# Attention decays of a decoder step, split into a high and a low part for the sums of later keys

## The chip, the cores and the metric

One core of one Trainium2 chip runs the whole step as one program. The metric is the device time of an execution in microseconds, as a median over runs; lower is better. The core has five engines with a queue each, worked off in order: TensorE (PE: matrix products, with its weight loads as PEld), VectorE (DVE), ScalarE (ACT), GpSimd (POOL) and SyncE (SP, which here only issues transfers). They meet only at semaphores: an instruction that waits holds up all that stand behind it in its queue. Transfers of all issuers run on the same 16 DMA engines.

## The reference, cut to what matters

The step has two layers with three sub-layers each. The change lies in the attention of the first layer's middle sub-layer: stick-breaking attention of 8 heads over 512 prompt tokens, computed in causal blocks of 128, and of 8 sample tokens over 512 cached keys.

```python
z = einsum('bqhd,bkhd->bhqk', qb, kb) * scale + bias
log_1m = where(mask, log_sigmoid(-z), 0.0)          # the decay of a key is -log_1m = softplus(z)
log_w = log_sigmoid(z) + cumsum(log_1m, axis=3, reverse=True) - log_1m
w = where(mask, exp(log_w), 0.0)
outs.append(einsum('bhqk,bkhd->bqhd', w, vb))
```

So a key's log weight is z less the sum of the decays of this key and all later ones that the query sees.

## The kernel before

A head's scores lie with the keys on the partitions and the queries along the free axis. Of the 4x4 blocks of 128 keys by 128 queries, 10 are causal, so a head is a tile of 128 x 1280 in four pieces: 512, 384, 256 and 128 columns for key block 0, 1, 2 and 3. Four such tiles hold scores (`ZS`: ZA to ZD) and four hold decays and later weights (`SP`: SA to SD); head h uses tile h % 4. The work goes in pairs of heads, t = 0 to 3.

What is done with a head, engine by engine:

- PE, `scores(t, j)`: products of keys and queries into PSUM bank 0, one piece j after the other.
- DVE, `scored` and `biased` (L1056): scale and bias into the tile in `ZS`. POOL, `masked` (L1223): the diagonal block's mask. DVE, `sized` (L1096): -|z| of the whole tile, from pair 1 on.
- ACT, `decay_of_pair` (L898): exp; after a change of function table, `log` (L902): ln(1 + x); after another change, `weights` of the pair before (L906).
- DVE, `softplus` (L1062): max(z, 0) plus that logarithm. The tile in `SP` now holds the head's decays, and semaphore `sp_done` says so.
- PE, `sums(h, i)` (L791, L794): for piece i, the product of the decays with the triangle `TRI` (keys of this block that are not before the key) and with `ONES` for each later block, summed in one of two halves of PSUM bank 1. Both operands are fp32. A half is taken again once DVE has read it (`lw_done`).
- DVE, `log_weights(h, i)` (L1069): z less the sum, in place. ACT, `weights(h)` (L906): exp into `SP`. PE, `values(t)` (L809): product with V for a pair. ACT, `outputs` (L952) and DVE, `low` (L1100): that product as a high part and a rest, since all large products of the program use operands of the kind float32r, split in two (weights: ACT L2142 makes the high part, DVE L2316 the rest; product L2030).

The loops at the end of `even_pe`, `even_act` and `even_dve` fix by hand in what order each engine does this. For each pair t the queue of ACT reads: outputs of pair t-1, the exps of pair t+1, table, the logarithms of pair t+1, table, the weights of heads 2t and 2t+1. Softplus(2t+2) and softplus(2t+3) stand on DVE among the log weights of head 2t+1. Heads 0 and 1 are started ahead of the loop.

Between these lie, on PE, the attention over cached values (`values_past`, L660, pages fetched by POOL, L1231), and 16 blocks of the adaLN product (L1964), two after each head of most, each of which needs a 512 KB tile AW that SP fetches when the block two before it is done (L633). SP also writes the new keys and the pooling rows out (`even_sp`, L625: 1 MB of keys, then 512 and 4096 pieces of 15 numbers), after it has asked for the first three units of the next stage ("evout").

## Time and profile before

| what | value |
|---|---|
| median of 3 runs | 2434.2 us (2428.53 to 2434.48) |
| span of the profiled execution | 2428.7 us |
| PE busy | 2382.6 us, 98% of the span |
| ACT busy, DVE busy | 995.2 us (41%), 1241.6 us (51%) |
| granted TensorE clock, mean | 0.996 of full |
| the stretch with the changed work | about 565 us to 656 us of the span |

The profiled execution stands at the lower end of the three runs, 5.5 us below their median. The page's view in 40 slices has PE at 9 tenths or more in all but the first and the last slice. Inside the attention stretch the shares differ: in the ten slices of 10 us from 560 to 660 PE is busy for 8.5 to 10.0 of 10 us, DVE for 3.0 to 7.6 and ACT for 2.5 to 8.2.

### The profile page before, as it was taken

What the parts mean: (1) busy time and instruction counts of PE and PEld (TensorE: products, weight loads), DVE (VectorE), ACT (ScalarE), POOL (GpSimd) and SP (SyncE); (2) the same over time, 40 slices, a digit from 0 to 9 for tenths busy, and PEclk for the clock granted to TensorE, in tenths of its full rate; (3) what the DMA queues carried; (4) which work ended last, traced back from release to release, by engine and by line L of the source; (5) the groups of instructions that cost most, each with busy time, mean ns of one, the idle gap of its engine ahead of it and who ended that gap; (6) DMA issues with size and microseconds to landing.
All of it is one profiled execution on the core that took longest, in us unless ns stands there. A gap on an engine that the chain in (4) does not pass through costs nothing.

```text
span 2428.7 us, 43792 instructions
## 1 busy us (share of the span) xinstructions
PE 2382.6 (98%) x18794; PEld 2185.1 (90%) x18794; DVE 1241.6 (51%) x1725; ACT 995.2 (41%) x1399; POOL 115.2 (5%) x232
## 2 busy tenths in 40 slices
PE   6999999999999999999999999999999999999998
PEld 5999999965599999999999999887777999999998
DVE  5533346755576333367533347755554758633245
ACT  4522234625466222346522235533223546522243
POOL 0000000122100000000000000012222100000000
PEclk9999999999999999999999999999999999999999
DMA  8555345774536653565754255544555455632254
GB/s 306 175 184 189 114 158 179 254 216 126 189 118 226 217 165 99 185 208 174 264 181 164 83 167 183 190 157 162 172 165 165 133 177 181 206 129 88 87 179 155
DMA packets 122658, 417.09 MB, mean 172 GB/s; under 512 B 23386, under 2 KB 27610, under 8 KB 122210
## 3 DMA queue, kind: packets, MB, share of 16 engines
q1 hardware_dynamic: 89538, 302.08, 38.8%
q10 hardware_dynamic: 17568, 61.87, 7.2%
q0 software_dynamic: 15360, 50.34, 6.3%
q8 instruction: 149, 2.44, 0.4%
q14 instruction: 43, 0.35, 0.0%
HBM read 390.84 MB, written 23.41 MB: 171 GB/s over the span
## 4 chain that ended last, share of the span: by engine, by line
PE 87%; DVE 5%; DMA 3%; ACT 3%; issue 2%; SPq 1%; POOLq 0%; POOL 0%; ACTq 0%; DVEq 0%
PE PS L2030 71%; PE PS L1425 3%; PE PS L1964 2%; PE PS L1994 2%; DVE WL L2316 2%; PE PS L1355 1%; DMA RAW<-in_w_in 1%; ACT WH L2142 1%; PE PS L1309 1%; PE PS L1340 1%; PE PS L1350 1%; PE PS L1321 1%; PE PS L791 1%; PE PS L1404 1%; PE PS L794 1%
## 5 line engine op out<-in xcount | busy, mean ns | idle before, releaser
L2316 DVE TENSOR_TENSOR WL<-RAW,WH 128x1024 fp32r<-128x1024 f32 (+1 forms) x478 | 633.1, 1325 | 648.7 <-ACT WH L2142 648.0
L2030 PE MATMUL PS<-HH,WH 128*128 128x260 f32 x3432 | 796.5, 285 | 2.4 <-ACT SG L2262 0.7
L2030 PE MATMUL PS<-HH,WL 128*128 128x260 f32 x3432 | 786.5, 283 | 0.0
L2030 PE MATMUL PS<-HL,WH 128*128 128x260 f32 x3368 | 769.6, 283 | 0.0
L2142 ACT ACTIVATE WH<-RAW 128x1024 fp32r<-128x1024 f32 (+1 forms) x478 | 542.0, 1135 | 424.7 <-PE PS L2030 264.9
L2030 PEld LDWEIGHTS PS<-HH,WH 128*128 128x128 f32 x3432 | 569.9, 188 | 24.7 <-issue 16.8
L2030 PEld LDWEIGHTS PS<-HH,WL 128*128 128x128 f32 x3432 | 569.4, 188 | 0.0
L2030 PEld LDWEIGHTS PS<-HL,WH 128*128 128x128 f32 x3368 | 557.0, 188 | 0.6 <-issue 0.2
L2030 PE MATMUL PS<-GH,WH 128*128 128x260 f32 x1408 | 386.1, 284 | 0.2
L2030 PE MATMUL PS<-GL,WH 128*128 128x260 f32 x1408 | 384.2, 283 | 0.0
L2030 PE MATMUL PS<-GH,WL 128*128 128x260 f32 x1408 | 383.5, 283 | 0.0
L2030 PEld LDWEIGHTS PS<-GH,WH 128*128 128x128 f32 x1408 | 259.0, 188 | 2.8 <-issue 2.6
L2030 PEld LDWEIGHTS PS<-GH,WL 128*128 128x128 f32 x1408 | 259.1, 188 | 0.0
L2030 PEld LDWEIGHTS PS<-GL,WH 128*128 128x128 f32 x1408 | 258.9, 188 | 0.2
L2265 ACT ACTIVATE GH<-SQ 128x260 fp32r<-128x260 f32 (+1 forms) x118 | 62.3, 528 | 374.1 <-DVE SQ L2486 374.1
L2486 DVE TENSOR_TENSOR SQ<-SG,PS 128x260 f32<-128x260 f32 (+1 forms) x118 | 65.6, 556 | 164.3 <-PE PS L2030 163.4
L2262 ACT ACTIVATE SG<-PS 128x260 f32<-128x260 f32 (+1 forms) x118 | 57.9, 491 | 219.2 <-PE PS L2030 215.9
L2475 DVE TENSOR_TENSOR GL<-SQ,GH 128x260 fp32r<-128x260 f32 (+1 forms) x118 | 66.3, 562 | 57.6 <-ACT GH L2265 56.9
L2030 PE MATMUL PS<-OGL,WH 128*128 128x260 f32 x256 | 69.6, 282 | 0.0
L1964 PE MATMUL PS<-AW,CSP 128*32 128x256 f32 x1024 | 66.9, 383 | 0.7 <-DMA AW<-in_w_ada 0.7
L1879 POOL DMA_DIRECT2D SR<-in_ret_past x32 | 18.3, 571 | 952.7 <-DVE WL L2316 929.3
L1964 PEld LDWEIGHTS PS<-AW,CSP 128*32 128x32 f32 x1024 | 30.4, 109 | 23.7 <-issue 2.3
(338 smaller groups left out, 2320.0 us busy)
## 6 DMA issues: line engine op xcount, KB each, us to landing
RAW<-in_w_in SPq DMA_DIRECT2D x236, 512.0 KB, 3.6
RAW<-in_w_out SPq DMA_DIRECT2D x120, 704.0 KB, 4.0
AW<-in_w_ada ACTq DMA_DIRECT2D x114, 512.0 KB, 5.6
RAW<-in_w_odd SPq DMA_DIRECT2D x60, 512.0 KB, 3.7
RAW<-in_w_odout SPq DMA_DIRECT2D x30, 512.0 KB, 3.8
RAW<-in_w_even SPq DMA_DIRECT2D x28, 512.0 KB, 4.3
KV<-in_v_pages POOLq DMA_DIRECT2D x32, 256.0 KB, 5.0
SR<-in_ret_past POOLq DMA_DIRECT2D x32, 256.0 KB, 3.9
```

What stands on the lines that cost most here:

```text
L791: last = nc.tensor.matmul(PS[1][:, i % 2, 0:LEN[i]], TRI[:], SP[h % 4][:, OFF[i]:OFF[i] + LEN[i]], start=True, stop=(i == 3))
L794: last = nc.tensor.matmul(PS[1][:, i % 2, (j - i) * P:LEN[i]], ONES[:], SP[h % 4][:, OFF[j]:OFF[j] + LEN[j]], start=False, stop=(j == 3))
L1425: last = nc.tensor.matmul(PS[tt // 2 if full else 0][:, tt % 2, :], src[k][:, tt // 2, (tt % 2) * P:(tt % 2 + 1) * P], w[:, w0:w0 + RV], s ...
L1964: last = nc.tensor.matmul(ADAP[CG * j:CG * j + CG, int(g == 1), 0:2 * P], CSP[:, k, :], w[:, 2 * P * j:2 * P * j + 2 * P], start=(k == 0), ...
L1994: last = nc.tensor.matmul(ps[:, x, 0:HT], w[:, k * P:(k + 1) * P], src[k][:, x, :], start=(start and k == 0), stop=(stop and k == KC - 1))
L2030: last = nc.tensor.matmul(ps[:, x, 0:HT], w[:, k * P:(k + 1) * P], src[k0 + k][:, x, :], start=(begin and t == 0), stop=(end and t == 2))
L2142: nc.scalar.activation(parts(p)[0], RAW[:, from_:from_ + w], ACT.Copy).then_inc(hi_done, 1)
L2262: nc.scalar.activation(SG[:, s, hs], PS[0][:, hs, 0:HT], ACT.Silu).then_inc(gate_evac, 1)
L2265: nc.scalar.activation(GH[:, r // 2, hs], G32[:, s, hs], ACT.Copy).then_inc(gh_done, 1)
L2316: nc.vector.tensor_tensor(low_, RAW[:, from_:from_ + w], high_.bitcast(F32), ALU.subtract).then_inc(lo_done, 1)
L2475: nc.vector.tensor_tensor(GL[:, r // 2, hs], G32[:, r // 2 % 2, hs], GH[:, r // 2, hs].bitcast(F32), ALU.subtract).then_inc(gl_done, 1)
L2486: nc.vector.tensor_tensor(G32[:, s, hs], SG[:, s, hs], PS[1][:, hs, 0:HT], ALU.mult).then_inc(up_evac, 1)
```

## The change

Each head's decays are written a second and a third time: ACT copies them to a tile of kind float32r (`high_part`, tiles SHA and SHB in turn), and DVE writes decays less high part, over the decays themselves and also as float32r (`low_part`). `sums` then makes each product twice, with the high and with the low part, both operands float32r: `TRIR` and `ONESR` are copies of the triangle and the ones, made once by ACT. The sums wait for `spl_done` (low part) where they waited for `sp_done` (softplus).

The tiles SHA and SHB take the place of the pooling inputs, so ACT's first high part waits until these are written out (`pool_out`), and SP writes them out before it asks for the first "evout" unit, not after the third. The four transfers have a semaphore of their own, so DVE no longer waits for the write of V before it fills ZC. OS, PSC and PT move to other addresses.

```diff
@@ even_sp
             for i in range(len(STEPS["evout"])):
-                if i == 3:
+                if i == 0:
                     sp.wait_ge(ev_act, EV_FULL)
                     sp.wait_ge(ev_dve, EV_FULL)
...
-                        sp.dma_start(dst, src).then_inc(out_done, 16)
+                        sp.dma_start(dst, src).then_inc(pool_out, 16)
+                if i == 3:
@@ even_pe, sums
                 if i == 0:
-                    pe.wait_ge(sp_done, h + 1)
+                    pe.wait_ge(spl_done, h + 1)
+                if h + i == 0:
+                    pe.wait_ge(const_ok, 3)
...
-                last = nc.tensor.matmul(PS[1][:, i % 2, 0:LEN[i]], TRI[:], SP[h % 4][:, OFF[i]:OFF[i] + LEN[i]],
-                                        start=True, stop=(i == 3))
-                for j in range(i + 1, 4):
-                    last = nc.tensor.matmul(PS[1][:, i % 2, (j - i) * P:LEN[i]], ONES[:],
-                                            SP[h % 4][:, OFF[j]:OFF[j] + LEN[j]], start=False, stop=(j == 3))
+                for j in range(i, 4):
+                    w = TRIR if j == i else ONESR
+                    for x, part in enumerate((SPH[h % 2], SPL[h % 4])):
+                        last = nc.tensor.matmul(PS[1][:, i % 2, (j - i) * P:LEN[i]], w[:],
+                                                part[:, OFF[j]:OFF[j] + LEN[j]], start=(j == i and x == 0),
+                                                stop=(j == 3 and x == 1))
@@ even_act
+            def high_part(h):
+                act.wait_ge(sp_done, h + 1)
+                if h == 0:
+                    act.wait_ge(pool_out, 64)
+                after(act, s_done, 4 * (h - 2) + 4)
+                nc.scalar.activation(SPH[h % 2], SP[h % 4], ACT.Copy).then_inc(sph_done, 1)
...
             table(EXP_SET)
+            act.wait_ge(kv_used, 4)
+            act.wait_ge(ident_ok, 4)
+            for dst, src in ((TRIR, TRI), (ONESR, ONES)):
+                nc.scalar.activation(dst[:], src[:], ACT.Copy).then_inc(const_ok, 1)
...
+            high_part(0)
             table(EXP_SET)
             decay(1)
...
-                for h in (2 * t, 2 * t + 1):
-                    weights(h)
+                if t == 0:
+                    high_part(1)
+                weights(2 * t)
+                if t < 3:
+                    high_part(2 * t + 2)
+                weights(2 * t + 1)
+                if t < 3:
+                    high_part(2 * t + 3)
@@ even_dve
+            def low_part(h):
+                dve.wait_ge(sph_done, h + 1)
+                nc.vector.tensor_tensor(SPL[h % 4], SP[h % 4], SPH[h % 2].bitcast(F32),
+                                        ALU.subtract).then_inc(spl_done, 1)
...
                     if t == 1:
-                        dve.wait_ge(out_done, 96)
+                        dve.wait_ge(pool_out, 64)
...
             nc.vector.tensor_tensor(ZN[:, 0, :], ZN[:, 0, :], PS[2][:, 0, :], ALU.subtract).then_inc(zn_dve, 1)
+            low_part(0)
             scored_one()
...
                 log_weights(2 * t, 1)
+                if t:
+                    low_part(2 * t + 1)
                 scored(t + 1, 2)
...
                 if t == 0:
                     softplus(1)
+                    low_part(1)
...
                 if t < 3:
                     softplus(2 * t + 3)
+                    low_part(2 * t + 2)
```

The queue of ACT around pair 0, before (SC_119 is the tile SC; L898 is an exp, L902 a logarithm, L906 a head's weights):

```order
L898 ACTIVATE SC_119<-SC_119 128x1280 [waits z_dve]
L898 ACTIVATE SD<-SD 128x1280 [waits z_dve]
L2166 ACT_TABLE_LOAD
L902 ACTIVATE SC_119<-SC_119,ONES 128x1280 [waits e_done]
L902 ACTIVATE SD<-SD,ONES 128x1280 [waits e_done]
L2166 ACT_TABLE_LOAD
L906 ACTIVATE SA<-ZA 128x1280 [waits lw_done]
L906 ACTIVATE SB<-ZB 128x1280 [waits lw_done]
```

And now (L909 is the exp, L913 the logarithm, L921 a high part, L925 the weights):

```order
L909 ACTIVATE SC_119<-SC_119 128x1280 [waits z_dve]
L909 ACTIVATE SD<-SD 128x1280 [waits z_dve]
L2208 ACT_TABLE_LOAD
L913 ACTIVATE SC_119<-SC_119,ONES 128x1280 [waits e_done]
L913 ACTIVATE SD<-SD,ONES 128x1280 [waits e_done]
L2208 ACT_TABLE_LOAD
L921 ACTIVATE SHB<-SB 128x1280 [waits sp_done]
L925 ACTIVATE SA<-ZA 128x1280 [waits lw_done]
L921 ACTIVATE SHA<-SC_119 128x1280 [waits s_done,sp_done]
L925 ACTIVATE SB<-ZB 128x1280 [waits lw_done]
L921 ACTIVATE SHB<-SD 128x1280 [waits s_done,sp_done]
```

The high part of head 1 (SHB<-SB) stands behind both exps, both logarithms and both table loads of pair 1, and those of heads 2 and 3 stand before and behind the weights of head 1.

The queue of DVE at the end of pair 0, before (L1062 is softplus, L1069 the log weights of a piece):

```order
L1062 SCALAR_TENSOR_TENSOR SB<-ZB,SB 128x1280 [waits z_dve,l_done]
L1069 TENSOR_TENSOR ZB<-ZB,PS 128x512 [waits s_done]
L1069 TENSOR_TENSOR ZB<-ZB,PS 128x384 [waits s_done]
L1062 SCALAR_TENSOR_TENSOR SC_119<-ZC,SC_119 128x1280 [waits z_dve,l_done]
L1069 TENSOR_TENSOR ZB<-ZB,PS 128x256 [waits s_done]
L1069 TENSOR_TENSOR ZB<-ZB,PS 128x128 [waits s_done]
L1062 SCALAR_TENSOR_TENSOR SD<-ZD,SD 128x1280 [waits z_dve,l_done]
```

And now (L1093 softplus, L1098 the low part, L1105 the log weights):

```order
L1093 SCALAR_TENSOR_TENSOR SB<-ZB,SB 128x1280 [waits z_dve,l_done]
L1098 TENSOR_TENSOR SBL<-SB,SHB 128x1280 [waits sph_done]
L1105 TENSOR_TENSOR ZB<-ZB,PS 128x512 [waits s_done]
L1105 TENSOR_TENSOR ZB<-ZB,PS 128x384 [waits s_done]
L1093 SCALAR_TENSOR_TENSOR SC_119<-ZC,SC_119 128x1280 [waits z_dve,l_done]
L1105 TENSOR_TENSOR ZB<-ZB,PS 128x256 [waits s_done]
L1105 TENSOR_TENSOR ZB<-ZB,PS 128x128 [waits s_done]
L1093 SCALAR_TENSOR_TENSOR SD<-ZD,SD 128x1280 [waits z_dve,l_done]
L1098 TENSOR_TENSOR SCL<-SC_119,SHA 128x1280 [waits sph_done]
```

A low part stands directly behind the softplus of head 1 and waits there for ACT; that of head 2 stands behind the softplus of head 3.

SP's queue, before and now in one piece:

```order
-L1916 DMA RAW<-in_w_evout 128x1024 [waits lo_done] x3
-L625 DMA out_k_t<-KP 128x2048 [waits ev_dve,ev_act]
-L625 DMA out_k_t<-QKVS 128x32
-L625 DMA out_pool_p<-UP 512x1x15
-L625 DMA out_pool_n<-US 4096x1x15
+L632 DMA out_k_t<-KP 128x2048 [waits ev_dve,ev_act]
+L632 DMA out_k_t<-QKVS 128x32
+L632 DMA out_pool_p<-UP 512x1x15
+L632 DMA out_pool_n<-US 4096x1x15
+L1957 DMA RAW<-in_w_evout 128x1024 [waits lo_done] x3
```

The four transfers now stand ahead of the three units of "evout".

## Rows read from the trace of the kernel before

**Rows 1.** The page: busy time, share and instructions; then shares of the chain that ended last.

```profile
PE 2382.6 (98%) x18794; PEld 2185.1 (90%) x18794; DVE 1241.6 (51%) x1725; ACT 995.2 (41%) x1399; POOL 115.2 (5%) x232
...
PE 87%; DVE 5%; DMA 3%; ACT 3%; issue 2%; SPq 1%; POOLq 0%; POOL 0%; ACTq 0%; DVEq 0%
```

**Rows 2.** Timeline of PE, sums of head 3: start us, us, engine, line, operation, form, count.

```profile
605.18 1.12 PE L791 MATMUL PS<-SD,TRI 128*128 128x512 f32 x2
...
609.87 0.38 PE L1976 MATMUL PS<-IDENT,ADS 128*128 128x128 f32 x2
```

**Rows 3.** Timeline of PE: neighbouring float32r products of 512 and of 260 columns.

```profile
538.14 0.39 PE L753 MATMUL PS<-WH,HH 128*128 128x512 f32 x1
538.37 0.39 PE L753 MATMUL PS<-WH,HL 128*128 128x512 f32 x1
...
657.39 0.28 PE L2030 MATMUL PS<-OHB,WH 128*128 128x260 f32 x1
657.51 0.28 PE L2030 MATMUL PS<-OLB,WH 128*128 128x260 f32 x1
```

**Rows 4.** The page: splitting a weight tile of 1024 columns (busy, mean ns of one).

```profile
L2316 DVE TENSOR_TENSOR WL<-RAW,WH 128x1024 fp32r<-128x1024 f32 (+1 forms) x478 | 633.1, 1325 | 648.7 <-ACT WH L2142 648.0
...
L2142 ACT ACTIVATE WH<-RAW 128x1024 fp32r<-128x1024 f32 (+1 forms) x478 | 542.0, 1135 | 424.7 <-PE PS L2030 264.9
```

**Rows 5.** Timeline of ACT: the weights of head 0, and the last table loads of pairs 1 and 2.

```profile
589.51 1.27 ACT L906 ACTIVATE SA<-ZA 128x1280 f32<-128x1280 f32 x1
...
610.03 1.28 ACT L2166 ACT_TABLE_LOAD   x1
...
632.04 1.28 ACT L2166 ACT_TABLE_LOAD   x1
```

**Rows 6.** Timeline of DVE: a softplus and the first steps of a later pair.

```profile
588.66 1.48 DVE L1062 SCALAR_TENSOR_TENSOR SC<-ZC,SC 128x1280 f32<-128x1280 f32 x1
...
601.34 1.51 DVE L1096 SCALAR_TENSOR_TENSOR SA<-ZA 128x1280 f32<-128x1280 f32 x1 [0.27 <-DVE ZB L1056]
...
623.35 1.51 DVE L1096 SCALAR_TENSOR_TENSOR SC<-ZC 128x1280 f32<-128x1280 f32 x1 [0.19 <-issue]
```

**Rows 7.** Timeline of PE: where heads 1, 2, 4 and 6 start their sums.

```profile
584.43 1.13 PE L791 MATMUL PS<-SB,TRI 128*128 128x512 f32 x2 [0.99 <-DVE SB L1062]
...
591.28 1.12 PE L791 MATMUL PS<-SC,TRI 128*128 128x512 f32 x2
...
611.37 1.10 PE L791 MATMUL PS<-SA,TRI 128*128 128x512 f32 x2
...
633.86 1.10 PE L791 MATMUL PS<-SC,TRI 128*128 128x512 f32 x2 [0.34 <-DVE ZB L1069]
```

**Rows 8.** Timelines of PE and SP, and a window with DMA share and GB/s last.

```profile
541.50 3.61 PE L646 MATMUL PS<-PAGE,QBM 128*16 128x512 f32 x16 [1.11 <-DMA PAGE<-in_k_pages]
...
532.87 1.11 SPq L625 DMA_DIRECT2D out_pool_n<-US  x1
...
542.00:544.00 2.00, 2.00 (x12) 0.51 (x10) 0.74 (x1) 0.00 (x0) 0.36 (x1) 1.00 1.69 102
```

**Rows 9.** Timeline of PE, and windows with the granted clock third from the end.

```profile
24.18 4.38 PE L1964 MATMUL PS<-AFIRST,CSP 128*32 128x256 f32 x48 [2.88 <-DMA AFIRST<-in_w_ada]
...
35.01 1.21 PE L1994 MATMUL PS<-HH,WH 128*128 128x260 f32 x4 [3.22 <-ACT HH L2201]
...
24.50:25.00 0.50, 0.50 (x8) 0.20 (x4) 0.00 (x0) 0.00 (x0) 0.00 (x0) 0.50 1.03 410
...
27.50:28.00 0.50, 0.50 (x16) 0.29 (x12) 0.00 (x0) 0.00 (x0) 0.00 (x0) 1.00 0.98 393
...
40.50:41.00 0.50, 0.50 (x4) 0.50 (x4) 0.06 (x1) 0.07 (x1) 0.00 (x0) 0.50 0.92 270
```

**Rows 10.** Timeline of PE: the adaLN block after head 6, and the next stage's first product.

```profile
642.49 0.64 PE L1964 MATMUL PS<-AW,CSP 128*32 128x256 f32 x8 [0.73 <-DMA AW<-in_w_ada]
...
656.21 0.39 PE L2030 MATMUL PS<-OHB,WH 128*128 128x260 f32 x1
```

More of the change, by code:

```diff
@@ L476, in decoder_step @@
         TRI = at("TRI", [P], g); g += size([P])
+        OS = at("OS", [4, NS], g); g += size([4, NS])
+        PSC = at("PSC", [4], g); g += 64
+        PT = at("PT", [NS * PAGES], g, I32); g += size([32])
         up_at = g
@@ L970, in even_act @@
             table(ROOT_SET)
-            act.wait_ge(out_done, 96)
+            act.wait_ge(pool_out, 64)
+            act.wait_ge(out_done, 32)
             for q, (n, hs) in enumerate(STEPS["evout"]):
@@ L1947, in _ @@
                 sp.dma_start(y_t[:, g:g + n, HT * x:HT * x + HT], X[:, g:g + n, x, :]).then_inc(y_out, 16)
-            sp.wait_ge(out_done, 96)
+            sp.wait_ge(pool_out, 64)
+            sp.wait_ge(out_done, 32)
             sp.wait_ge(rp_out, 32 * RH)
```

28 lines of the change are left out of this document (16 added, 12 removed).

## The prediction, made before the changed kernel ran

> **What bounds the kernel now.** I read the page first. PE is busy 98% of the span and makes 87% of the chain that ended last, with 5% on DVE and 3% on ACT [rows 1]. So over the whole program a shorter product is worth its time. Then I took the attention stretch apart with the timelines of PE, DVE and ACT side by side, since there a head passes through all three before PE can take its sums. What the reader should see there is how narrow PE's lead is: head 1's sums start after 0.99 us idle for a softplus, head 6's after 0.34 us idle for DVE [rows 7]. Each head's sums begin almost as soon as its decays are there. Whatever is put between softplus and sums lies on the path at once.
>
> **What is taken from PE.** The sums of head 3 run without a wait from 605.18 to 609.87, 4.69 us for 2560 columns [rows 2]; fp32 products show as two instructions each (x2). A float32r product of 512 columns takes 538.37 - 538.14 = 0.23 us, one of 260 columns 0.12 us [rows 3], so 0.45 ns per column. High and low part make 5120 columns: 2.3 us. A head gains 4.69 - 2.3 = 2.4 us of PE, eight heads 19 us. No row has a float32r product under 260 columns, and the sums have 8 of 128 columns per head. Bounds: 0.06 us (in proportion to columns) up to 0.12 us, what 260 columns take; times 64 such products that is 0 to 3.8 us over all heads, and also a price beyond that can't be excluded. I take 0.1 us each, most of which falls into time in which PE waits anyway: 0.5 us on the path.
>
> **What is put on ACT and DVE.** High part: ACT reads and writes 1280 elements per partition; the weights of a head, of that size, take 1.27 us [rows 5]. Low part: a DVE operation of two inputs with 1280 elements takes 1.48 us [rows 6]; splitting a weight tile of 1024 costs 1.14 us on ACT and 1.33 us on DVE in the page's mixed means [rows 4], so both are near 1.3 and 1.5 us. Eight of each are 10 us of ACT and 12 us of DVE. Between them lie only semaphores, some 0.05 us each. If everything stood free, a head's sums would start 1.3 + 1.5 = 2.8 us later. But the queues decide. I walked them pair by pair, with rows' durations and the new order.
>
> Head 0. The copies of V end at 566.9, the high part ends near 568.2 and the low part near 569.7. It stands ahead of the four scalings of head 1, which go back by 1.6 us. The wait for the write of V that DVE no longer has gives back 0.8 us, and PE's shorter sums absorb the rest: softplus(1) ends where it did, near 584.3. The 2.4 us of head 0 are gone. The copies of triangle and ones (two of 128 columns, under 0.3 us each) fall into 0.6 us in which ACT waits for DVE; without that cover they would cost 0.5 us.
>
> Head 1. Its decays are ready at 584.4 [rows 7]. But its high part stands behind the exps, table, logarithms and table of pair 1, and ACT is free at 589.5 [rows 5]. High part until 590.8, low part until 592.3: the sums start at 592.3 and not 584.4, **7.9 us late**. Behind DVE's wait stand the log weights of head 1 and the softplus of heads 2 and 3, so these can't run ahead either.
>
> Pair 1. softplus(2) started at 588.66 [rows 6], 4.2 us after head 1's sums; with shorter sums this becomes 2.7 us, so 595.0. softplus(3) follows 2 us later and ends near 598.4, then DVE makes low(2) until 599.9, and head 2's sums start at 599.9 instead of 591.28 [rows 7]: 8.7 us late.
>
> Pair 2. The first -|z| of head 4 was at 601.34 [rows 6], 10.1 us after head 2's sums. The gain of PE there is eaten by low(3), 1.4 us ahead of two scalings: 609.8, 8.5 us late. ACT follows this through exps, table, logarithms and table, which ended at 610.03 + 1.28 = 611.3 [rows 5], now 619.8. Before the high part of head 4 come the weights of head 2: 1.2, then 1.3 and 1.5 us for high and low part. Head 4's sums start near 623.8 instead of 611.37 [rows 7]: **12.4 us late**.
>
> Pair 3. The same: the -|z| of head 6 (623.35 [rows 6], 12.0 us after head 4's sums) comes 11 us after them, since copies that held it up now fall into PE's wait: 11.5 us late. The table load that ended at 632.04 + 1.28 = 633.3 [rows 5] ends at 644.8, plus 1.2 + 1.3 + 1.5 gives 648.8 for head 6's sums instead of 633.86 [rows 7]: **15 us late**.
>
> The end. From there PE needed 22.4 us to the next stage at 656.21 [rows 10]. Two heads save 4.8 us, less 1.4 us for low(7), and PE waits for the adaLN tile, 0.73 us now [rows 10], some more then, since the tile's transfer doesn't get shorter. Net 2.8 us back: **+12.2 us**. The wait that takes the place of the one on softplus is thus about 8 us at head 1, 2 at head 2, 5 to 6 at heads 4 and 6.
>
> **The transfers that move.** Keys and pooling rows are written from about 516 us instead of 531, ahead of two "evout" units and against the 16 cached key pages. The last pages now make PE wait 1.11 us [rows 8]. While the small rows are written (issued at 532.87), the DMA share is 1.69 and only 102 GB/s move [rows 8]. That stretch would come earlier by 15 us, while pages are still under way: bounds -1.1 us (the wait goes away, the 1 MB of keys being gone earlier) and +5 us. I take +2 us, nearer to the row's 1.11 us. The waits for `pool_out` are then long fulfilled (568 and 572 us), and the "evout" units aren't needed before 656 us. The edits of addresses cost nothing.
>
> **PE's clock.** Twice the trace has PE idle for about 3 us: 2.88 us and 3.22 us [rows 9]. At 24.5 the granted clock is 0.50, the lower level (1.2 GHz), and at 27.5 it is 1.00 (2.4 GHz); behind the second gap it still is 0.50 at 40.5, some 5.5 us after PE began again. The attention stretch now never has a gap of more than 1.5 us. The three new gaps of 5 to 8 us are longer than both of these. A gap would then bring 3 to 6 us at half clock, in which 1.5 to 3 us of PE's work are lost, in part beside work of DVE: bounds 0 and 9 us for three; I take 3.5 us. The Trainium skill speaks against this change here (TensorE: Matmul & The Clock Gate, "HAM oscillation — how this bites in real kernels"): short work between waits leaves the array to start slow again behind each wait. By that rule all three gaps pay and the term is nearer its upper bound, by the attention stretch as it stands it would be 0.
>
> **The sum.** 12.2 + 0.5 + 2 + 3.5 = 18.2 us. The profiled span of 2428.7 us becomes 2446.9; that execution stood 5.5 us below the median of 2434.2 us, and against the median the forecast is **2452 us**, +0.75%. About 0.3%, 7 us, is what a measurement of this kernel can tell from no change.
>
> **The rivals.**
> 1. The clock stays at its upper level, and the pages land in time: 12.2 us or a little more, 2447 us. For it: 1.00 throughout the stretch now. Against it: rows 9. Chance 0.18; slower all the same.
> 2. The clock stays low through most of the stretch, or short float32r products cost as much per column as fp32: 2.4 us per head fall to about 1.1 us in the first case of it, and all PE work of some 40 us costs more. 10 us on top of the forecast: 2462 us. Chance 0.12. The extreme of it is that the change doesn't do what it says, and float32r isn't cheaper in the sums at all: then 19 us of PE's work come back, most of them on the path by then: 2468 us. It is within this chance.
> 3. The delay is paid once. The 7.9 us at head 1 come from a place in ACT's queue that returns at no other head, and ACT idles before each pair's exps. If pairs 2 and 3 find enough slack, the sums of the other heads give 7 x 2.4 = 17 us against 7.9 + 2: 2427 us, faster. It decides at head 4: the loop from its softplus to its sums must take under 2 us, where I have 1.2 + 1.3 + 1.5. Against it: weights and both parts are in series there. Chance 0.05.
> 4. Half of that: some waits overlap with adaLN blocks and pages, and head 4 and 6 lose only what PE gains: 2434 + 5 us. Chance 0.09.
>
> **How the numbers follow.** Forecast 0.56, rivals 0.18, 0.12, 0.05 and 0.09. Range: 2440 us, between rival 4 and rival 1, to 2463 us, with most of rival 2. Faster by more than 0.3% is rival 3: 0.05. Within 0.3%, 2427 to 2441 us, is rival 4 and the lower edge of rival 1: 0.10. Slower: 0.85.
>
> **What would show it.** In the changed kernel's timeline of PE: head 3's sums take 2.4 us and not 4.69; PE idles near 584 to 592 for a low part; head 4's and head 6's sums each follow a gap of 5 us; ACT's high part of head 1 starts where its weights of head 0 started. DVE's low part takes 1.4 to 1.5 us and ACT's high part 1.2 to 1.3. The granted clock falls to 0.50 behind the gap at head 1. The stage behind attention starts 15 to 20 us later, and the rest of the program is only shifted. Wrong is the forecast if head 1's sums start before 588 us, or if the shift at head 4 is smaller than the one at head 1.

## The result, and where the time went

The changed kernel takes 2466.5 us (median of 4 runs, 2465.4 to 2470.4) against 2434.3 us (2428.5 to 2436.3, 4 runs) of the kernel before: 1.0147 times, 95% interval 1.0135 to 1.016. That is 32 us slower, in the direction forecast, but 14.5 us above the forecast of 2452 and outside its range. One of the 29 executions of the kernel before that ran beside experiments 9 to 12 fell into a slower state of the chip (2581.11 us at a granted clock of 0.849) and enters no interval or range below.

The page of the changed kernel, busy time and chain, to be set beside [rows 1]: PE is busy for nearly as long (2383.9 and 2382.6 us), and the chain has more of DVE and ACT, and names a page transfer that it did not name before.

```profile
PE 2383.9 (97%) x18794; PEld 2187.5 (89%) x18794; DVE 1252.1 (51%) x1733; ACT 1004.8 (41%) x1409; POOL 114.9 (5%) x232
...
PE 85%; DVE 6%; ACT 4%; DMA 3%; issue 2%; SPq 0%; POOLq 0%; POOL 0%; ACTq 0%; DVEq 0%
PE PS L2072 69%; PE PS L1466 3%; PE PS L2006 2%; PE PS L2036 2%; DVE WL L2358 2%; PE PS L1396 1%; ACT WH L2184 1%; DMA RAW<-in_w_in 1%; DMA KV<-in_k_pages 1%; PE PS L1350 1%; PE PS L1381 1%; PE PS L1391 1%; PE PS L804 1%; PE PS L1362 1%; ACT Y L2235 1%
```

That PE's busy time is nearly the same is a sum of two changes: the sums have shorter products, and part of the program ran at the lower clock (mean 0.987 against 0.996), where the same products take longer.

**The first half of the loss lies ahead of the attention stretch.** PE's timeline, products of the cached key pages (L654):

```profile
542.14 5.54 PE L654 MATMUL PS<-KV,QBM 128*16 128x512 f32 x16 [13.96 <-DMA KV<-in_k_pages]
...
556.47 3.62 PE L654 MATMUL PS<-PAGE,QBM 128*16 128x512 f32 x16
```

The last set starts at 556.47 and not at 541.50 [rows 8]: 14.97 us late, behind 13.96 us in which PE has nothing to do. The set behind that wait took 5.54 us where 3.61 is usual, since it ran at the lower clock: 1.9 us of the 15 are the clock's, and the wait of 1.11 us that stood ahead of the last set is gone. Windows of that place (granted clock, DMA share and GB/s last), and the DMA issues between 500 and 560 us (KB each, median us from issue to landing):

```profile
520.00:530.00 10.00, 8.18 (x33) 5.33 (x31) 2.20 (x3) 2.43 (x3) 3.93 (x8) 1.00 1.46 135
530.00:540.00 10.00, 0.00 (x0) 0.00 (x0) 0.53 (x1) 0.00 (x0) 1.96 (x4) 0.62 1.36 79
540.00:550.00 10.00, 7.86 (x25) 2.15 (x26) 0.50 (x1) 0.69 (x1) 0.54 (x1) 0.70 0.94 352
```
```profile
KV<-in_k_pages POOLq DMA_DIRECT2D x8, 256.0 KB, 7.8
PAGE<-in_k_pages POOLq DMA_DIRECT2D x8, 256.0 KB, 16.7
KV<-in_v_pages POOLq DMA_DIRECT2D x8, 256.0 KB, 3.2
...
out_pool_n<-US SPq DMA_DIRECT2D x1, 240.0 KB, 23.2
```

While the 240 KB of small pieces are written, for 23 us, the 16 engines are busy beyond 1.3 in share and move 79 to 135 GB/s, and a page needs 16.7 us. In the kernel before the same issues read:

```profile
KV<-in_k_pages POOLq DMA_DIRECT2D x8, 256.0 KB, 3.4
PAGE<-in_k_pages POOLq DMA_DIRECT2D x8, 256.0 KB, 3.7
KV<-in_v_pages POOLq DMA_DIRECT2D x8, 256.0 KB, 11.3
```

There it was the value pages that were slow (11.3 us), for which nobody waited.

**The second half is the attention stretch.** PE's timeline, first products of the sums of heads 0, 1, 2, 4 and 6, and the next stage's first product, to be set beside [rows 7, 10]:

```profile
589.22 0.79 PE L804 MATMUL PS<-SHA,TRIR 128*128 128x512 f32 x1
...
609.23 0.79 PE L804 MATMUL PS<-SHB,TRIR 128*128 128x512 f32 x1 [8.97 <-DVE SBL L1098]
...
618.71 0.51 PE L804 MATMUL PS<-SHA,TRIR 128*128 128x512 f32 x1 [2.08 <-DVE SCL L1098]
...
642.82 0.79 PE L804 MATMUL PS<-SHA,TRIR 128*128 128x512 f32 x1 [3.88 <-DVE SAL L1098]
...
669.53 0.79 PE L804 MATMUL PS<-SHA,TRIR 128*128 128x512 f32 x1 [2.77 <-DVE SCL L1098]
...
691.62 0.39 PE L2072 MATMUL PS<-OHB,WH 128*128 128x260 f32 x1
```

Counted from the end of the page products (start of the last and its duration: 560.09 us, before 545.11), the shifts are 9.8 us at head 1 (24.80 less 14.98), 12.5 at head 2, 16.5 at head 4, 20.7 at head 6 and 20.4 us at the next stage. The spans differ by 36.3 us: 15.0 for the pages, 20.4 for attention, 0.9 for all the rest of the program.

How far can one trace be trusted to a microsecond? Experiments 1, 3, 4 and 10 below leave attention as it was. Their heads 0 to 6 start within 0.05 us of where they start in the kernel before, counted in this way (head 6: 88.72 to 88.75 us). Between heads 6 and 7 they differ, by how long PE waits for the adaLN tile (0.73 us in the kernel before [rows 10], 0 to 0.22 in the others), and the next stage begins after 110.1 to 110.6 us, not 111.1. So attention lost 20.4 to 21.4 us.

The queues of ACT and DVE at head 1 are as the order of instructions says. ACT:

```profile
605.09 1.28 ACT L2208 ACT_TABLE_LOAD   x1
606.38 1.27 ACT L921 ACTIVATE SHB<-SB 128x1280 fp32r<-128x1280 f32 x1
```

DVE (low part, log weights, softplus of head 2):

```profile
607.68 1.49 DVE L1098 TENSOR_TENSOR SBL<-SB,SHB 128x1280 fp32r<-128x1280 f32 x1 [6.44 <-ACT SHB L921]
611.87 0.69 DVE L1105 TENSOR_TENSOR ZB<-ZB,PS 128x512 f32<-128x512 f32 x1 [2.70 <-PE PS L804]
613.37 0.56 DVE L1105 TENSOR_TENSOR ZB<-ZB,PS 128x384 f32<-128x384 f32 x1 [0.81 <-PE PS L804]
613.84 1.48 DVE L1093 SCALAR_TENSOR_TENSOR SC<-ZC,SC 128x1280 f32<-128x1280 f32 x1
```

The high part starts with the end of the table load, DVE waits 6.44 us for it, and PE 8.97 us for both.

### The profile page after: what moved, and what is told of

Its sections match the earlier page's. It is cut to its first block, busy times and chain, and to the rows that moved or that the text cites. A ratio compares the mean times of both kernels' runs of the same rounds, so it can differ in the third digit from the quotient of the medians.

```text
span 2465.0 us, 43819 instructions
## 1 busy us (share of the span) xinstructions
PE 2383.9 (97%) x18794; PEld 2187.5 (89%) x18794; DVE 1252.1 (51%) x1733; ACT 1004.8 (41%) x1409; POOL 114.9 (5%) x232
## 4 chain that ended last, share of the span: by engine, by line
PE 85%; DVE 6%; ACT 4%; DMA 3%; issue 2%; SPq 0%; POOLq 0%; POOL 0%; ACTq 0%; DVEq 0%
PE PS L2072 69%; PE PS L1466 3%; PE PS L2006 2%; PE PS L2036 2%; DVE WL L2358 2%; PE PS L1396 1%; ACT WH L2184 1%; DMA RAW<-in_w_in 1%; DMA KV<-in_k_pages 1%; PE PS L1350 1%; PE PS L1381 1%; PE PS L1391 1%; PE PS L804 1%; PE PS L1362 1%; ACT Y L2235 1%
## 5 line engine op out<-in xcount | busy, mean ns | idle before, releaser
L2184 ACT ACTIVATE WH<-RAW 128x1024 fp32r<-128x1024 f32 (+1 forms) x478 | 542.1, 1135 | 432.9 <-PE PS L2072 265.2
L1920 POOL DMA_DIRECT2D SR<-in_ret_past x32 | 18.2, 570 | 954.6 <-DVE WL L2358 931.1
```

Source lines behind the costliest of these rows:

```text
L2184: nc.scalar.activation(parts(p)[0], RAW[:, from_:from_ + w], ACT.Copy).then_inc(hi_done, 1)
```

## The experiments

All are compared with the kernel before, run beside them: 2430.25 us for experiments 1 to 4 (7 runs), 2432.18 us for 5 to 8 (13), 2431.58 us for 9 to 12 (29). The times of that kernel alone lie between 2428 and 2438 us, so differences of 1 to 3 us are read from the traces. The second column of numbers is the median less that of the kernel before run beside it; experiments of different groups are best compared by it. Then come two places of each trace: where the last page products end, and how much later the next stage begins. The first of the two is good to some 2 us only: the first page products of the stage, ahead of the place of the changes, start at 506.8 to 510.3 us.

| kernel | median us | median less that of before | pages end | to next stage |
|---|---|---|---|---|
| before (profiled execution: span 2428.7) | 2434.3 | | 545.1 | 111.1 |
| changed | 2466.5 | 32.2 | 560.1 | 131.5 |
| e1 move of the transfers alone | 2446.1 | 15.9 | 560.8 | 110.2 |
| e2 changed, transfers in their old place | 2454.5 | 24.2 | 547.8 | 133.6 |
| e3 only the keys moved (one run) | 2440.0 | 9.8 | 554.7 | 110.1 |
| e4 only the pooling rows moved (one run) | 2442.8 | 12.5 | 557.5 | 110.6 |
| e5 as e2, PE's waits filled | 2450.3 | 18.1 | 544.0 | 132.2 |
| e6 as e2, other queue places | 2448.9 | 16.7 | 546.8 | 125.0 |
| e7 before, float32r sums without parts | 2428.7 | -3.5 | 548.6 | 110.6 |
| e8 as e2, fp32 sums (one run) | 2461.0 | 28.8 | 544.7 | 140.2 |
| e9 changed, pooling rows packed | 2452.5 | 21.0 | 543.5 | 131.7 |
| e10 before, packed | 2429.4 | -2.2 | 545.3 | 110.1 |
| e11 packed, parts for head 7 alone | 2427.7 | -3.9 | 542.1 | 109.0 |
| e12 parts for head 7 alone | 2430.0 | -1.6 | 545.9 | 109.3 |

### The transfers that move: experiments 1 to 4 and 9

Two theories: the moved transfers alone stall the pages; or they cost little, as predicted, and the stall came with the splitting.

```diff
             for i in range(len(STEPS["evout"])):
-                if i == 3:
+                if i == 0:
                     sp.wait_ge(ev_act, EV_FULL)
                     sp.wait_ge(ev_dve, EV_FULL)
...
-                        sp.dma_start(dst, src).then_inc(out_done, 16)
+                        sp.dma_start(dst, src).then_inc(pool_out, 16)
+                if i == 3:
```

> The kernel before, and only the four transfers (keys of the prompt, keys of the samples, two sets of pooling rows) written out ahead of the first unit of the next stage, as in the changed kernel; nothing is split. Theory: the move alone holds up the cached key pages; the third set of page products starts about 15 us late (556.5 us and not 541.5), behind a wait of some 14 us, and the time is 2434 + 15 = 2449 us. Rival (as in the prediction): it costs -1.1 to 5 us, 2433 to 2439 us, and the stall in the changed kernel came from what the splitting does to the queues.

Measured: 2446.1 us (2444.0 to 2447.3), 1.0058 times (1.0039 to 1.0077). PE's timeline has the stall of the changed kernel, with nothing split:

```profile
542.00 6.33 PE L646 MATMUL PS<-KV,QBM 128*16 128x512 f32 x16 [15.27 <-DMA KV<-in_k_pages]
557.13 3.62 PE L646 MATMUL PS<-PAGE,QBM 128*16 128x512 f32 x16
```

The last page products start 15.6 us late, the span is 15.2 us longer, and attention itself takes 110.2 us, as in the kernels that leave it alone. So the first theory holds: the move costs this by itself. The converse is the changed kernel with the four transfers back behind the third unit:

> The changed kernel with the four transfers back behind the third unit. Theory: the stall ahead of the page products is gone and the rest stays: 2466.5 - 15 = 2451.5 us, within 2 us. Rival: without the stall other waits of the attention stretch grow, since the logarithms there had caught up meanwhile: 2455 us or more. In the attention stretch head 1's sums still start 9 to 10 us late against the kernel before, head 6's 20 us.

Measured: 2454.5 us (2451.4 to 2455.8), 1.0089 times (1.007 to 1.0108). The long stall is gone; a short one is left, and behind it the products ran at the lower clock (5.31 us for what takes 3.61):

```profile
542.46 5.31 PE L652 MATMUL PS<-PAGE,QBM 128*16 128x512 f32 x16 [2.73 <-DMA PAGE<-in_k_pages]
...
597.19 0.79 PE L802 MATMUL PS<-SHB,TRIR 128*128 128x512 f32 x1 [8.97 <-DVE SBL L1096]
```

12 us came back and not 15, so the time lies outside the theory's 2451.5 within 2 us and just below the rival's 2455 us. The traces say why. The pages end 12.3 us earlier: 1.6 us of the 2.7 that are missing are the longer wait (2.73 us, not 1.11), and 1.7 us the lower clock behind it (this execution was 0.7 us ahead at the first page products). This stall is not the work of the change: of the kernels with the transfers in their old place and the rows not packed, three show a wait of 2.6 to 2.7 us here with half clock behind it (experiments 2, 6 and 7) and four one of 0.9 to 1.3 us without (before, 5, 8, 12). And attention took 133.6 us, not 131.5. The rival has the sign right, but not the reason: in experiment 9, where the long stall is gone too, attention takes 131.7 us. In experiment 2 the clock fell to 0.50 behind head 2's wait of 2.24 us, and by head 3 PE was 1.8 us behind (75.9 against 74.2 us from the page products). In the changed kernel and in experiment 9 it stayed at 1.00 behind waits of 2.08 and 1.99 us at the same place.

What of the four transfers is it? One set moved at a time, the other left (the diff is that of experiment 1 with two of the four in each place):

> The kernel before, with only the two transfers of keys (1 MB and 128 rows) moved ahead; the pooling rows stay. If the 1 MB of keys takes the DMA time of the pages: a stall of 3 us and more at the page products, up to the whole 14 us. If it is the 4608 pieces of 60 bytes: at most the 1.11 us that the kernel before has.

> The kernel before, with only the pooling rows (4608 pieces of 15 numbers) moved ahead; the keys stay. If the small pieces hold the pages up: a stall of 10 us and more at the third set of page products. If the keys do: none above 2 us.

Each move alone stalls the pages. Experiment 3 fits neither theory as I had written it: I had not thought that moved keys could bring the pages together with pieces that stay. Experiment 3, then experiment 4:

```profile
549.74 4.91 PE L650 MATMUL PS<-PAGE,QBM 128*16 128x512 f32 x16 [8.52 <-DMA PAGE<-in_k_pages]
```
```profile
539.57 5.48 PE L650 MATMUL PS<-KV,QBM 128*16 128x512 f32 x16 [12.09 <-DMA KV<-in_k_pages]
```

With the small pieces moved, the stall comes at 527 to 540 us, as in the changed kernel. With the keys moved, it comes at 541 to 550 us, though the small pieces leave from their old place. By the expectation as written, 8.52 us would speak for the keys' own 1 MB. Windows of 2 us say otherwise (DMA share and GB/s last; the kernel before, then experiment 3):

```profile
536.00:538.00 2.00, 2.00 (x9) 1.30 (x8) 0.00 (x0) 0.34 (x1) 0.90 (x2) 1.00 0.99 416
```
```profile
536.00:538.00 2.00, 2.00 (x10) 1.47 (x8) 0.00 (x0) 0.00 (x0) 1.07 (x2) 1.00 2.15 53
```

In the kernel before the larger set of small pieces is issued at 532.87 us [rows 8], but behind 1 MB of keys, and throughput stays above 250 GB/s until 542 us, by when the last page, issued at 531.29 us, has landed (PE starts on that set at 541.50). In experiment 3 nothing stands ahead of the pieces: they are issued at 531.22 us, and throughput is at 53 GB/s from 536 us on. The last page is issued only 1.5 us later than before (532.8 us). So the keys, ahead of the small pieces, had held these back by some 5 us, just enough for the pages; that the moved keys push the pages back (a key page lands in 5.3 us, not 3.4) seems the smaller part, though no run separates the two. Either way, keys without small pieces would cost nearly nothing. Experiment 9 tries it in the changed kernel: GpSimd copies the rows into a tile PK without gaps, in idle time, and the write has 256 pieces of 240 and 1920 bytes. PK lies where V comes later, so the first copy of V waits for `pool_out`.

```diff
+                if q == 2:
+                    pool.wait_ge(ev_act, AHEAD["evin"] + 4)
+                    pool.wait_ge(ev_dve, AHEAD["evin"] + 4)
+                    nc.gpsimd.tensor_copy(PK[:, 0:60].rearrange("p (a c) -> p a c", c=15),
+                                          UP[:, :, SEQ + 1:SEQ + 16]).then_inc(ident_ok, 1)
+                    nc.gpsimd.tensor_copy(PK[:, 60:540].rearrange("p (a b c) -> p a b c", a=4, b=NS),
+                                          US[:, :, :, 1:16]).then_inc(ident_ok, 1)
...
-                                     (pool_p, UP[:, :, SEQ + 1:SEQ + 16]), (pool_n, US[:, :, :, 1:16])):
+                                     (pool_p.rearrange("p a c -> p (a c)"), PK[:, 0:60]),
+                                     (pool_n.rearrange("p a b c -> p (a b c)"), PK[:, 60:540])):
```

> The changed kernel, transfers still ahead of the first unit, but GpSimd first copies the two sets of pooling rows into one tile without gaps (in time in which it is idle), so that they leave as 256 pieces of 240 and 1920 bytes and not as 4608 of 60 bytes. Theory: the small pieces are what holds the pages up, in whichever place; with them gone the move costs 2 us at most, the third set of page products starts at 541 to 543 us, and the time is 15 us less than that of the changed kernel, 17 us above before: 2450 us. Rival: the 1 MB of keys ahead of the pages costs most of it: a stall of 8 us and more stays, 2458 us or more.

Measured: 2452.5 us (2449.6 to 2453.9), 1.0089 times (1.0074 to 1.0103). The copies take 0.23 and 0.59 us on POOL. PE waits 1.46 us at one place, and issue to landing is short again:

```profile
527.42 3.61 PE L657 MATMUL PS<-KV,QBM 128*16 128x512 f32 x16 [1.46 <-DMA KV<-in_k_pages]
```
```profile
KV<-in_k_pages POOLq DMA_DIRECT2D x8, 256.0 KB, 5.8
PAGE<-in_k_pages POOLq DMA_DIRECT2D x8, 256.0 KB, 4.5
...
out_pool_n<-PK SPq DMA_DIRECT2D x1, 240.0 KB, 8.2
```

Same place in the queue, same bytes, and the stall of 14 us is gone: it was that the bytes left in so many and so small pieces, and the rival, the 1 MB of keys, is ruled out. The attention stretch takes 131.7 us, as in the changed kernel (131.5). The gain against the changed kernel is 14.0 us, or 11.2 us by the differences to the kernels run beside; 21.0 us above before, where the theory had 17, is what the longer attention stretch alone costs.

### The price of the queues and of the clock: experiments 5, 6 and 8

Theory: the splitting costs by its places in the queues of ACT and DVE, plus some half-clock time of PE. The rival for the first part is that the float32r sums gave back all their PE time and the queues cost even more; experiment 8 takes the gain away and leaves the queues:

```diff
-                    for x, part in enumerate((SPH[h % 2], SPL[h % 4])):
-                        last = nc.tensor.matmul(PS[1][:, i % 2, (j - i) * P:LEN[i]], w[:],
...
+                    last = nc.tensor.matmul(PS[1][:, i % 2, (j - i) * P:LEN[i]], (TRI if j == i else ONES)[:],
+                                            SPH[h % 2].bitcast(F32)[:, OFF[j]:OFF[j] + LEN[j]], start=(j == i),
```

> The changed kernel with the transfers in their old place, high and low parts made and waited for as there, but the sums as one fp32 product each, of the high part alone. Theory: the queue then costs its whole price and PE gives nothing back: some 7 us more than with float32r sums, 2461 us, and not 17 to 19 us more. Rival: the float32r sums gave back all of their 17 us: 2472 us.

Measured: 2461.0 us (one run), 6.5 us above experiment 2 (4.6 us by the differences to before); by the traces 140.2 against 133.6 us, 6.6 us, and against the 131.5 us of the changed kernel 8.7 us. So the shorter products give back some 7 to 9 us, and the rival's 2472 us is far off. The parts cost 140.2 - 111.1 = 29 us in all, the clock's share among them; this rests on one trace.

Experiment 5 fills PE's waits with products whose results are overwritten, so that it is at work there too:

```diff
                 pe.wait_ge(lw_done, n - 1) if n >= 2 else pe.wait_ge(vp_evac, 4)
+                if i == 0:
+                    filler(FILL[h])
+                    pe.wait_ge(spl_done, h + 1)
...
+            FILL = (0, 7, 1, 0, 3, 0, 2, 0)
+                    nc.tensor.matmul(PS[1][:, 0, :], TRI[:], QP[:, 0, :], start=True, stop=True)
```

> The changed kernel with the four transfers in their old place, and with products that fill PE's waits for a low part: 7 of 512 columns fp32 ahead of head 1's sums, 1, 3 and 2 ahead of those of heads 2, 4 and 6, 1 among the scores of head 1. They write a half of PSUM bank 1 that the sums then overwrite, and their results are not used. Theory: the low level of the clock behind each wait costs some 4 to 6 us, of which most comes back: 2454.5 - 5 = 2449.5 us, with the granted clock at 1.00 in the attention stretch. Rival: the half-clock work lies beside waits for ACT and DVE anyway, and the time stays within 2 us of 2454.5.

Measured: 2450.3 us (2448.7 to 2453.6), 1.0069 times (1.0052 to 1.0087). That is near the theory's 2449.5 us, but the intervals of this and of experiment 2 overlap, and the two profiled executions differ by 3.8 us before attention begins, for the short stall told above, so the medians decide nothing. In the traces, counted from the page products, head 4 starts at 81.2 us with filling and at 84.4 us without. But the clock was not held: 2.77 us of wait at head 1 were left, and the first product behind it still takes 0.79 us, where 0.50 us is that of the upper level; and head 6 met something else:

```profile
591.81 0.79 PE L813 MATMUL PS<-SHB,TRIR 128*128 128x512 f32 x1 [2.77 <-DVE SBL L1107]
...
625.16 0.50 PE L813 MATMUL PS<-SHA,TRIR 128*128 128x512 f32 x1 [1.82 <-DVE SAL L1107]
...
652.97 1.08 PE L2015 MATMUL PS<-AW,CSP 128*32 128x256 f32 x8 [4.14 <-DMA AW<-in_w_ada]
```

PE came to the adaLN block earlier, the tile's transfer ran beside eight value pages, and PE waited 4.14 us for it (0.54 us in experiment 2). What was gained by head 4, 3.2 us, was mostly lost there: 1.5 us are left at the next stage. Nor are the 3.2 us the clock's price in the changed kernel. 1.8 of them are the fall at head 2, which experiment 2 had and the changed kernel had not; there head 4 starts at 82.7 us without any filling. So filling is worth 1.5 us up to head 4 against that kernel, 3.2 against experiment 2, and less than the whole price, since the clock still fell. The price over the whole stretch stays open.

Experiment 6 changes only places in the queues: softplus(1) ahead of `sized(1, 0)`, high_part(1) ahead of the exps of pair 1, both high parts of a pair ahead of both weights, low_part(2t+3) right behind low_part(2t+2).

```diff
+                if t == 0:
+                    high_part(1)
                 if t < 3:
                     decay_of_pair(t + 1)
...
-                if t == 0:
-                    high_part(1)
-                weights(2 * t)
                 if t < 3:
                     high_part(2 * t + 2)
-                weights(2 * t + 1)
-                if t < 3:
                     high_part(2 * t + 3)
+                weights(2 * t)
+                weights(2 * t + 1)
```

> The changed kernel with the transfers in their old place and other queue places: softplus of head 1 ahead of the -|z| of pair 1 on DVE, its high part ahead of the exps of pair 1 on ACT; on ACT the high parts of both heads of a pair ahead of the two weights; on DVE the low part of an odd head right behind that of the even one. Theory: the queue's share is some 13 to 16 us, and these places give back 7 to 8 of it, and 1 to 3 of clock, since the wait at head 1 falls from 9 us to under 4: 2445 us. Rival: the loop from softplus to sums is what costs, not the places: 2452 us or more. Slower than before either way.

Measured: 2448.9 us (2447.1 to 2450.5), 1.0064 times (1.0047 to 1.0081). It lies between the theory's 2445 us and the rival's 2452. In the trace the stretch falls from 133.6 to 125.0 us, 8.6 us (6.5 against the changed kernel), of which head 1 makes most (its sums start 42.7 us behind the page products, not 49.4):

```profile
589.53 0.50 PE L802 MATMUL PS<-SHB,TRIR 128*128 128x512 f32 x1 [2.28 <-DVE SBL L1095]
...
602.07 1.65 PE L691 MATMUL PS<-QP,KP 64*128 64x384 f32 x4 [2.19 <-DVE ZB L1084]
...
624.75 0.79 PE L802 MATMUL PS<-SHA,TRIR 128*128 128x512 f32 x1 [4.37 <-DVE SAL L1095]
```

The wait at head 1 is 2.28 us instead of 8.97. The first product behind it still ran at the upper level of the clock (0.50 us), but the granted clock was 0.50 from 590.5 to 593.5 us: the fall came a microsecond later, and was not avoided. The wait at head 4 is not shorter (4.37 us): there the loop itself, from softplus through both parts to the sums, is too long for this order too; other orders were not tried. So places explain about a third of the loss in attention, 6.5 to 8.6 us.

### How much the shorter products could bring at all: experiment 7

```diff
+                for j in range(i, 4):
+                    w = TRIR if j == i else ONESR
+                    for x in range(2):
+                        last = nc.tensor.matmul(PS[1][:, i % 2, (j - i) * P:LEN[i]], w[:],
+                                                SPL[h % 4][:, OFF[j]:OFF[j] + LEN[j]], start=(j == i and x == 0),
...
-                nc.vector.scalar_tensor_tensor(SP[h % 4], ZS[h % 4], 0.0, SP[h % 4], ALU.max,
+                nc.vector.scalar_tensor_tensor(SPL[h % 4], ZS[h % 4], 0.0, SP[h % 4], ALU.max,
```

> The kernel before with the sums as two float32r products each, but with no work on ACT and DVE for it: the softplus writes the decays as float32r, and both products take this one tile, against a triangle and ones of 0.5. It leaves out the low part, so the decays have less precision. Theory: PE's work falls by about 17 us, but DVE's and ACT's chain between the heads takes most of its place: 4 us faster than before, 2426 us. Rival (what the change counts on): PE is the bound all along, and all of it comes back: 2413 us.

Measured: 2428.7 us (2427.0 to 2433.9, 10 runs), 0.9985 times (0.9976 to 0.9995): 3.5 us faster (1.2 to 5.8 by the interval), and the rival's 2413 us is excluded. With no price at all on ACT and DVE, the changed sums would have brought a few microseconds of the 12 to 19 by which PE's work is shorter. The trace can't say where they come from: its execution was the slowest of the ten (2433.9 us), and attention takes 110.6 us in it, no less than with fp32 sums. Part of the rest is lost where ACT's weights of head 1, then DVE's scaling, hold up PE's scores (ACT, DVE, PE):

```profile
593.68 1.25 ACT L913 ACTIVATE SB<-ZB 128x1280 f32<-128x1280 f32 x1
```
```profile
594.96 0.75 DVE L1066 TENSOR_SCALAR ZA<-PS,BIAS 128x512 f32<-128x512 f32 x1 [1.34 <-ACT SB L913]
```
```profile
596.43 0.92 PE L689 MATMUL PS<-QP,KP 64*128 64x384 f32 x4 [2.17 <-DVE ZB L1066]
```

DVE waits for ACT and PE for DVE. The clock takes its share too: behind this wait it was at 0.50 from 598 to 601 us, and once more behind a wait of 3.04 us for DVE at head 4 (granted clock third from the end):

```profile
620.00:625.00 5.00, 5.00 (x20) 1.71 (x16) 1.14 (x2) 0.00 (x0) 0.59 (x2) 0.50 0.05 18
```

How much each takes is not told apart.

### A kernel that beats both: experiments 10 to 12

Head 7's decays are ready long before its sums (its table load ends 9.7 us before them in the kernel before), and no later head hangs on it. Experiment 12 is experiment 2 with both parts for head 7 alone; 10 is the kernel before with the packing of experiment 9; 11 has both.

```diff
             def high_part(h):
+                if h not in [7]:
+                    return
...
+                    if h not in [7]:
+                        last = nc.tensor.matmul(PS[1][:, i % 2, (j - i) * P:LEN[i]], (TRI if j == i else ONES)[:],
+                                                SP[h % 4][:, OFF[j]:OFF[j] + LEN[j]], start=(j == i), stop=(j == 3))
+                        continue
```

> The kernel before, with the same packing of the pooling rows, transfers in their old place, nothing split. Theory: the wait of 1.1 to 2.7 us for the last key pages and the products at half clock behind the longer of them go away: 2 to 4 us faster than before, 2428.5 us. Rival: the wait moves to another page set or to the pages of values, no difference.

> The packing, transfers in their old place, and high and low part for head 7 alone, whose decays are ready long before its sums; the other heads' sums are fp32 as before. Theory: head 7's float32r sums give 1.6 us on top of the packing, since both its parts lie in idle time of ACT and DVE and no queue loop hangs on them: 2427 us. Rival: they hold up the log weights of head 6 and give nothing: the time of packing alone.

> The changed kernel with the transfers in their old place and high and low part for head 7 alone, without the packing. Theory: 1.6 us faster than before: 2430.5 us. Rival: no gain or up to 2 us slower.

Measured: 2429.4 us (0.9993 times, 0.9984 to 1.0001), 2427.7 us (0.9987, 0.9978 to 0.9996) and 2430.0 us (0.9993, 0.9982 to 1.0003). By median the three are 2.2, 3.9 and 1.6 us faster than before; only for the second does the interval exclude no difference, so the rival of experiment 10, no gain, is not excluded by its times. All three lie near their theories (2428.5, 2427 and 2430.5 us). The traces tell what of it is the packing and what head 7. The wait ahead of the last page products (1.11 us [rows 8]) is gone with the packing, and the way from the first page products to the end of the last is 1.2 us shorter in experiments 10 and 11. Attention with packing alone takes 110.1 us; that it is 1.0 us less than before is the adaLN tile's wait, which experiments 1 and 3 have lost without any packing. From the start of head 7's sums to the next stage it is 13.16 us in the kernel before and in experiment 10, and 11.6 to 11.7 in experiments 11 and 12: 1.5 us less. The sums start 0.4 us later in 11 than in 10, so 1.1 us are left. Experiment 11, end of the stretch: head 7's parts are ready, and its sums wait only 0.34 us for a half of PSUM.

```profile
639.44 0.47 PE L809 MATMUL PS<-SHB,TRIR 128*128 128x512 f32 x1 [0.34 <-DVE ZC L1116]
...
651.08 0.39 PE L2090 MATMUL PS<-OHB,WH 128*128 128x260 f32 x1
```

## Why the prediction was wrong, step by step

**The step that failed is the term of the transfers that move: +2 us, bounds -1.1 and +5, against 15.0 us measured.** I had named the right place and taken its price from the wrong number: the wait of 1.11 us [rows 8] is what the small pieces cost when they meet the last pages only. The other number of the same group would have given it. At 102 GB/s the eight pages of one set, 2.1 MB, take some 20 us; at the 285 GB/s that flowed in the ten microseconds ahead (520 to 530 us of the kernel before) they take 7 us; the difference is 13 us, an estimate made after the fact, and its closeness is in part luck, since the 102 GB/s hold small pieces as well as pages. It also leaves out the 1.9 us that the clock took behind the stall, a fourth gap that I had not put into the term for the clock. I looked at how long PE waited, not at how long the resource was slow and who would stand in that time after the move. Experiments 1 and 9 show the term alone, put in and taken out: 15.2 us of span, and the page products done at 543.5 us, 36.6 us behind the first of them, where it is 36.2 in the kernel before and 51.0 in the changed one.

**The queue walk held, and was a little short.** Forecast shifts 7.9, 8.7, 12.4 and 15 us at heads 1, 2, 4 and 6, measured 9.8, 12.5, 16.5 and 20.7. The mechanism at each place is as told: the high part of head 1 behind ACT's tables, parts of 1.27 and 1.49 us (forecast 1.3 and 1.5), waits of 8.97 and 2.08 us at heads 1 and 2 (forecast 8 and 2). At heads 4 and 6 the waits are 3.88 and 2.77 us and not 5 to 6, though the heads start later than forecast: PE's own work between them took longer. The missing part has three pieces.

- Head 0, put at nothing: +2.5 us by the start of its sums (589.22 less the 14.98 of the pages is 574.24; before 571.77). Low(0) ahead of the scalings lets PE wait 1.69 us, and the scores behind it ran at half clock (2.08 us where 1.13 stood). 1.9 us of this reach head 1, by way of DVE's -|z| and ACT's exps of pair 1: the table load ahead of the high part ends at 606.37, less 14.98 that is 591.4, where I had 589.5. That is the whole miss at head 1.
- The sums of a head were forecast at 2.3 us. Head 3 at full clock, first product, first product of the second piece, and the work behind the sums:

```profile
634.25 0.50 PE L804 MATMUL PS<-SHB,TRIR 128*128 128x512 f32 x1
...
635.57 0.39 PE L804 MATMUL PS<-SHB,TRIR 128*128 128x384 f32 x1
...
637.47 0.41 PE L2018 MATMUL PS<-IDENT,ADS 128*128 128x128 f32 x2
```

  That is 3.2 us instead of 4.69 [rows 2]: a gain of 1.5 and not 2.4 us. The short products are not the reason: those of 128 columns follow each other by 0.06 us (635.40 and 635.46), in proportion. Between the pieces PE now waits for DVE to empty a half of PSUM: DVE is done with the first two pieces near 636.5 and 637.13, and the third and fourth start at 636.51 and 637.19.
- At head 1 the lower clock made the sums 5.3 us long (609.23 to 614.50). Softplus(2) came 4.6 us behind their start, where I had 2.7. The gain I had counted for head 1 was not there.

**The clock** was forecast at 3.5 us for three gaps. Windows of the changed kernel around head 1, and around head 4 (granted clock third from the end):

```profile
600.00:610.00 10.00, 1.03 (x6) 0.68 (x3) 2.73 (x2) 8.75 (x7) 4.31 (x8) 0.70 0.85 277
610.00:620.00 10.00, 7.92 (x48) 6.25 (x46) 7.29 (x9) 3.59 (x3) 0.29 (x1) 0.78 0.46 143
...
640.00:650.00 10.00, 7.18 (x29) 3.98 (x29) 6.08 (x10) 3.55 (x4) 2.77 (x7) 0.66 0.45 141
```

The kernel before had 1.00 in all of them. It fell behind the wait of 9 us and also behind those of 3 to 4 us, as the 0.79 us of the first products of heads 4 and 6 show. I had counted those three gaps at 5 to 8 us. The Trainium skill's rule that spoke against the change (TensorE: Matmul & The Clock Gate, "HAM oscillation — how this bites in real kernels") agrees with that. The size of the term stays open: experiment 5, whose filling was incomplete, gives 1.5 to 3.2 us up to head 4, where the 3.5 us were meant for all three gaps, and the price at head 0 and behind the page stall was in no term.

**The sum.** 18.2 us forecast for the span, 36.3 measured: 13.0 for the transfers, 4.2 in attention (20.4 against 16.2), 0.9 elsewhere. Against the medians it is 32 and not 36 us, since the profiled span of before stood 5.6 us under the median and that of the changed kernel 1.5 us under its own. Rival 1 fell with the clock and with the pages; rival 2, with 2462 us nearest to the result, has another reason, and float32r products did cost a quarter of fp32; rivals 3 and 4 fell with head 4. Of the signs that I named, the wait at head 1, the two parts' durations and the clock behind head 1 came true. Head 3's sums took 3.2 us and not 2.4, the gaps at heads 4 and 6 were shorter than 5 us, and the stage behind attention starts 35 us later and not 15 to 20.

## What to carry to other kernels

When a transfer is moved, price it by the time in which it slows the engines and by what will be under way then, not by the wait that it causes where it stands now. A saving on the busiest engine is worth what the loop through its neighbours leaves of it: at least 1.5 us of products in each of eight heads were worth 3.5 us here even for free, and a step of 1.3 + 1.5 us put into the loop of every head cost 29 us, the clock included. Where one transfer stands ahead of another in a queue, it also decides when the other begins: see what it holds back before it is moved. Put such a split where the result waits anyway (the last head), and copy ragged rows together before writing them out.

## What the runs showed of the hardware

- 4608 pieces of 60 bytes, 270 KB: the larger set of 4096 lands 22 to 26 us after its issue (experiments 1 to 4 and the changed kernel); windows of 10 us in that time move 46 (experiment 4) to 135 GB/s, where 285 flow without them. In 256 pieces the larger set lands in 8.2 us. The Trainium skill (DMA: Bandwidth & Descriptors, "Why small descriptors are slow (HBM only)") gives a fixed overhead of a few cycles for each packet and 32 bytes of metadata for each operation; the direction agrees, the size here is far larger: 23.2 us x 16 engines for the 4096 pieces of the second set are, as an estimate, 90 ns a piece, at most, since other transfers went on beside them.
- A write that nobody waits for can be the costliest transfer: it moves the wait to whoever reads beside it (13.96 us for the pages here).
- Small pieces issued behind 1 MB of the same queue slow the others only once this is through: throughput falls near 542 us for an issue at 532.87, and at 536 us for one at 531.22 with nothing ahead (experiment 3).
- float32r products of 128 columns follow each other by 0.06 us, in proportion to the 0.23 us of 512; an fp32 product takes some four times as long (0.96 us for 512 columns [rows 2], 605.18 to 606.14 us, against 0.23).
- The lower level of the clock also follows short waits, and not each time: waits of 2.24 us (experiment 2) and 2.08 us (changed kernel) at the same place were followed by 0.50 and by 1.00. In experiment 6 PE waits 2.23 us at head 2 and 2.19 us some 3.7 us later, and then the scores of 384 columns take 1.65 us, which take 0.92 us at the upper level (596.43 us of experiment 7).
